# In a state-space scan, the carried part of a chunk is turned by two transposes ahead of its 64-column matmuls

## The chip, the cores and the metric

The kernel runs on one core of a Trainium2 chip. The core has engines that run side by side and meet only at semaphores: TensorE (PE in the profile, with PEld for its weight loads), VectorE (DVE), ScalarE (ACT), GpSimd (POOL) and SyncE (SP). The metric is the time of one execution on the device in microseconds (us); lower is better.

## The reference, cut to what matters

Two model blocks stand one behind the other: a two-layer block with differential attention, a linear recurrence and an MLP, then a block with a state-space scan over 768 tokens (256 of context, 512 latent) and an attention layer. The change is in the scan, which works in chunks of 128 tokens, in both directions of time:

```python
def ssd_scan(xs, dt, a, bm, cm, init_state, need_y=True):
    ...
    la_cum = jnp.cumsum(dtc * a, axis=2)
    to_end = jnp.exp(la_cum[:, :, -1:] - la_cum) * dtc
    states = jnp.einsum('bcsgn,bcsgr,bcsgrp->bcgrpn', bc, to_end, xc)
    chunk_decay = jnp.exp(la_cum[:, :, -1])

    def step(carry, inp):
        st, dec = inp
        return carry * dec[..., None, None] + st, carry

    final, prev = lax.scan(step, init_state.astype(F32), ...)
    ...
    cb = jnp.einsum('bclgn,bcsgn->bclsg', cc, bc)
    w = cb[..., None] * decay * dtc[:, :, None]
    y_diag = jnp.einsum('bclsgr,bcsgrp->bclgrp', w, xc)
    y_off = jnp.einsum('bclgn,bcgrpn,bclgr->bclgrp', cc, prev, jnp.exp(la_cum))
    return (y_diag + y_off).reshape(xs.shape), final
```

`y_off` is the carried part: what earlier chunks' states give to this chunk. `y_diag` is the part from within the chunk. There are 8 groups of 4 heads, each head 64 wide, and 6 chunks.

## The kernel before, in words

Every engine has its own program, in an order written out by hand. TensorE multiplies float32 data; the large products are made of float32r halves (`whi`, `wlo` and `inhi`, `inlo`), each product of them one pass, with three passes for one result. GpSimd splits each 1 MB weight tile into its halves (L337 and L341) as soon as TensorE is done with the tile that stood in that slot.

The scan runs over the 8 groups in `group(g, last)`: seven times in a hardware loop, and once more with `last` set. A group begins with a dense product for its gate (`zs`), then turns the convolved inputs of the 6 chunks (L692 to L694), makes the chunk states (L724), and goes through the 6 chunks. For each chunk c TensorE's order is: half a dense product for the next group (`next_half`, 24 matmuls of L628), the log decays of chunk c + 1 (L733, L735), `y_part(c)` (L757, L761), and the carried part of chunk c + 1 (`off_part`, L746). The last group has no next group, so its chunks have no dense product between them. Behind the chunks stand the output products of the group (`out_block`, again L628).

`y_part(c)` fills the 256 columns of one half of PSUM bank 7: two halves b of 128 columns, each 128 partitions high, where partitions 0 to 63 and 64 to 127 belong to two heads r. It waits for three semaphores: `offs_r` (the carried part of the chunk is in `offs`, laid out by token), `W_r` (the decay weights `wdec`) and `y_rd` (the bank's half was read). Then for each b it multiplies `offs` by the identity, a float32 product, which turns it from token rows to feature rows, and adds for each head r a product of 64 output partitions and 128 columns, `xcb` with `wdec`.

VectorE works in the order `gate_y(c - 1)` (L1926, reads bank 7), `offsets(c)` (L1917 to L1920, makes `offs`), `weights(c)` (L1903, L1907, makes `wdec`), with pieces of the next group's convolution (L1804, L1808), its activation (`silu`, L1822) and `skip` (L1899) placed among them. After chunk 5 it goes through `u_lo` (L1935), the remaining convolution, the eight additions to the output (`out_add`, L1997) and two sums of squares (L2002), and ends with `silu` of the last of four convolution blocks. TensorE may turn the next group's inputs (L692) only after that one.

Of the kernel before, what the change touches and what calls it, by code (L numbers as in the profile page):

```python
# [24 lines left out]
P = 128  # L25
# [69 lines left out]
def build(nc, io, stage=2):  # L95
# [258 lines left out]
    def _(pe):  # L354
# [74 lines left out]
        with pe.Fori(0, DEPTH) as l:  # L429
# [118 lines left out]
            b = 0  # L548
# [16 lines left out]
            for g in range(4):  # L565
                banks_wait(g % 2, ("pp_r", g + 1))
                for m in range(2):
                    n = 0
                    for kb in range(2):
                        c = kb * D + (2 * g + m) * P  # L570
                        for x, y in ((whi, phi), (wlo, phi), (whi, plo)):
                            mm = pe.matmul(ps[:, 2 * (g % 2) + m, :], x[:, T_PP % 2, c:c + P], y[:, kb, :],  # L572
                                           start=(n == 0), stop=(n == 5))
# [86 lines left out]
        for d, tri in enumerate((triF, triB)):  # L660
# [3 lines left out]
                  start=True, stop=True).then_inc(dt_p, 1)  # L664
        dense(T_BC0 % 2, lambda i: i * TM + P, P, IN, EIGHT, True, 0, lambda: pe.wait_ge(x_rd, 2))

        def group(g, last):
# [16 lines left out]
            for c in range(NC):  # L684
                q = 4 + c % 4
# [64 lines left out]
            def y_part(c):  # L750
                pe.wait_ge(offs_r, g * 6 + (c + 1))
                pe.wait_ge(W_r, g * 6 + (c + 1))
                pe.wait_ge(y_rd, g * 6 + (6 + c))
                base = (c % 2) * 256
                for b in range(2):
                    q = base + b * P
                    pe.matmul(ps[:, 7, q:q + P], offs[:, 0, 2 * b:2 * b + 2, :].rearrange("p r n -> p (r n)"), ident[:, :],  # L757
                              start=True, stop=False)
                    for r in range(2):
                        x0 = (2 * b + r) * HD  # L760
                        mm = pe.matmul(ps[64 * r:64 * r + 64, 7, q:q + P], xcb[:, c, x0:x0 + HD], wdec[:, 2 * b + r, :],  # L761
                                       start=False, stop=True)
                mm.then_inc(y_ps, 1)

            log_decay(0)
# [2 lines left out]
            for c, (name, part) in enumerate((("x0", 1), ("x1", 0), ("x1", 1), ("b", 0), ("b", 1), ("c", 0))):  # L768
                next_half(name, part)
                if c + 1 < NC:  # L770
                    log_decay(c + 1)
                y_part(c)
                if c + 1 < NC:
                    off_part(c + 1)
# [34 lines left out]
        for half in range(2):  # L809
            mm = pe.matmul(ps[:, 6 + half, 0:HALF], ones[:, :], acc[:, half * HALF:(half + 1) * HALF],  # L810
                           start=True, stop=True)
# [12 lines left out]
        for c in range(NC):  # L824
# [3 lines left out]
            for kb in EIGHT:  # L828
                for i, (a, w) in enumerate(((inhi, whi), (inhi, wlo), (inlo, whi))):
                    mm = pe.matmul(ps[:, 4 + c % 4, 0:TM], a[:, kb, cs], w[:, (T_ATT + 1) % 2, kb * TM:(kb + 1) * TM],  # L830
                                   start=(kb == 0 and i == 0), stop=(kb == KB - 1 and i == 2))
# [52 lines left out]
        for m in range(2):  # L884
            for half in range(2):
                mm = pe.matmul(ps[:, 4 + 2 * m + half, 0:HALF], bones[:, :], ksq[:, m, half * HALF:(half + 1) * HALF],
                               start=True, stop=True)
# [1533 lines left out]
```

## Time and profile before

| | |
|---|---|
| median of 3 runs | 2689.7 us (2688.63 to 2698.87) |
| the profiled execution | 2686.75 us |
| its span, first to last instruction | 2685.0 us |
| PE busy | 2454.4 us (91%) |
| DVE busy | 1433.8 us (53%) |
| POOL busy | 1308.4 us (49%) |
| ACT busy | 798.6 us (30%) |
| mean granted TensorE clock | 0.97 of full speed |

Times within the profile count from the start of the span. A float32 matmul that is a true product appears as two records, one for each pass; a float32 transpose appears as one. The duration of a record runs until its last result is out and overlaps with the records behind it, so what an instruction costs a stream of others is read from the distance between starts. In a row of the timeline, `x4` says that four neighbouring records of one kind are drawn together, and what stands in brackets is the engine's idle time ahead of it and what ended it.

### The profile page before, as it was taken

Reading aid. Unit: us, or ns where it says so; the run is one execution under the profiler, and the core shown is the slowest. Engines: PE = TensorE matmul, PEld = TensorE weight load, DVE = VectorE, ACT = ScalarE, POOL = GpSimd, SP = SyncE. Lnnn points to the kernel's source line nnn. Section 1 sums busy time; section 2 is a strip of 40 time slices with the busy share of each in tenths; the row PEclk is TensorE's granted clock in tenths of the full one; section 3 lists DMA queues with packets and bytes.
Section 4 is the critical chain, followed back from the end, with each engine's and each line's share of the span. In section 5 each row is a group of like instructions: output and inputs, shape, how many; then the busy total and the mean of one; then the engine's idle time right before and its main releaser. Section 6 shows DMA issues by size and latency. Waiting matters only on the chain.

```text
span 2685.0 us, 36345 instructions
## 1 busy us (share of the span) xinstructions
PE 2454.4 (91%) x13296; PEld 2033.1 (76%) x13296; DVE 1433.8 (53%) x1780; ACT 798.6 (30%) x1700; POOL 1308.4 (49%) x1220
## 2 busy tenths in 40 slices
PE   5989999999798899999977799999999997798997
PEld 4657888888665688888856698988898885676876
DVE  7574311114675541121356787778788786326762
ACT  2233110112222420011223333233333332325771
POOL 5734766667784276666762242443434341253003
PEclk9999999999899999999989899999999997999999
DMA  4211334432221034443231010110111112021001
GB/s 145 72 58 48 111 127 139 141 121 100 95 77 65 30 106 128 137 141 130 98 124 56 32 48 31 47 47 31 47 47 47 47 39 82 16 94 48 2 1 47
DMA packets 33839, 201.44 MB, mean 75 GB/s; under 512 B 4416, under 2 KB 6592, under 8 KB 13632
## 3 DMA queue, kind: packets, MB, share of 16 engines
q1 hardware_dynamic: 23328, 164.13, 17.5%
q10 hardware_dynamic: 10400, 35.73, 4.2%
q8 instruction: 82, 1.34, 0.2%
q14 instruction: 29, 0.24, 0.0%
HBM read 194.60 MB, written 5.24 MB: 74 GB/s over the span
## 4 chain that ended last, share of the span: by engine, by line
PE 82%; DVE 9%; ACT 4%; issue 3%; POOL 1%; DMA 0%; ACTq 0%; SPq 0%; DVEq 0%; POOLq 0%
PE ps L385 40%; PE ps L628 19%; PE ps L848 5%; PE ps L746 2%; PE ps L761 1%; PE ps L757 1%; PE ps L605 1%; PE ps L724 1%; PE ps L929 1%; PE ps L408 1%; PE ps L946 1%; PE ps L572 1%; PE ps L493 1%; ACT tin L1190 1%; PE ps L733 1%
## 5 line engine op out<-in xcount | busy, mean ns | idle before, releaser
L337 POOL TENSOR_SCALAR whi<-wraw 128x512 fp32r<-128x512 f32 x608 | 407.7, 698 | 1352.2 <-PE ps L628 628.2
L341 POOL TENSOR_TENSOR wlo<-wraw,whi 128x512 fp32r<-128x512 f32 x608 | 905.8, 1520 | 0.0
L385 PE MATMUL ps<-uhi,whi 128*128 128x512 f32 x960 | 383.9, 400 | 49.3 <-DVE ulo L1497 40.4
L385 PE MATMUL ps<-uhi,wlo 128*128 128x512 f32 x960 | 376.9, 393 | 0.0
L385 PE MATMUL ps<-ulo,whi 128*128 128x512 f32 x960 | 376.3, 392 | 0.0
L628 PE MATMUL ps<-inhi,whi 128*128 128x384 f32 (+1 forms) x816 | 258.2, 353 | 44.9 <-DVE inlo L1752 27.9
L385 PEld LDWEIGHTS ps<-uhi,whi 128*128 128x128 f32 x960 | 182.2, 190 | 94.8 <-issue 48.0
L628 PE MATMUL ps<-inhi,wlo 128*128 128x384 f32 (+1 forms) x816 | 246.1, 338 | 0.0
L628 PE MATMUL ps<-inlo,whi 128*128 128x384 f32 (+1 forms) x816 | 245.9, 338 | 0.0
L1670 DVE TENSOR_TENSOR h<-h,ps 128x1024 f32<-128x1024 f32 x40 | 48.9, 1221 | 306.4 <-PE ps L385 306.4
L385 PEld LDWEIGHTS ps<-uhi,wlo 128*128 128x128 f32 x960 | 182.3, 190 | 38.6 <-issue 1.9
L385 PEld LDWEIGHTS ps<-ulo,whi 128*128 128x128 f32 x960 | 182.0, 190 | 38.6
L385 PE MATMUL ps<-hidhi,whi 128*128 128x512 f32 x512 | 202.2, 395 | 0.0
L385 PE MATMUL ps<-hidhi,wlo 128*128 128x512 f32 x512 | 199.5, 390 | 0.0
L385 PE MATMUL ps<-hidlo,whi 128*128 128x512 f32 x512 | 199.3, 389 | 0.0
L628 PEld LDWEIGHTS ps<-inhi,whi 128*128 128x128 f32 (+1 forms) x816 | 150.8, 189 | 54.7 <-issue 40.4
L1282 ACT ACTIVATE ebuf<-ps,tabg 128x128 f32<-128x128 f32 x384 | 104.2, 383 | 170.7 <-PE ps L735 117.2
L628 PEld LDWEIGHTS ps<-inhi,wlo 128*128 128x128 f32 (+1 forms) x816 | 152.2, 190 | 2.1
L1687 DVE SCALAR_TENSOR_TENSOR hm<-ps,rstd 128x1024 f32<-128x1024 f32 x32 | 39.1, 1223 | 212.0 <-PE ps L385 212.0
L628 PEld LDWEIGHTS ps<-inlo,whi 128*128 128x128 f32 (+1 forms) x816 | 151.6, 189 | 0.9
L1808 DVE SCALAR_TENSOR_TENSOR convd<-raw,cpg,convd 128x770 f32<-128x770 f32 x128 | 146.3, 1143 | 2.3
L1131 ACT ACTIVATE hsq<-hm 128x1024 f32<-128x1024 f32 x32 | 34.0, 1061 | 296.5 <-DVE hm L1687 296.5
(369 smaller groups left out, 4519.0 us busy)
## 6 DMA issues: line engine op xcount, KB each, us to landing
wraw<-in_wstream SPq DMA_DIRECT2D x152, 1024.0 KB, 4.9
modraw<-in_modw ACTq DMA_DIRECT2D x48, 512.0 KB, 3.6
hspill<-hres ACTq DMA_DIRECT2D x1, 3072.0 KB, 9.4
hback<-hspill ACTq DMA_DIRECT2D x1, 3072.0 KB, 10.1
h<-in_x SPq DMA_DIRECT2D x1, 2048.0 KB, 7.4
out<-hfin SPq DMA_DIRECT2D x2, 1024.0 KB, 4.0
gw<-in_gates ACTq DMA_DIRECT2D x2, 512.0 KB, 5.3
pT<-in_pT ACTq DMA_DIRECT2D x2, 512.0 KB, 6.0
```

Of the source, the lines that this page charges most:

```text
L337: pool.tensor_scalar(whi[:, s, c], wraw[:, s, c], 1.0, 0.0, ALU.mult, ALU.add).then_inc(wraw_read, 1)
L341: ins = pool.tensor_tensor(wlo[:, s, c], wraw[:, s, c], whi[:, s, c].bitcast(F32), ALU.subtract)
L385: mm = pe.matmul(ps[:, 2 * bank + m, :], a[:, w, c:c + P], b[:, kb, :], start=(n == 0 and i == 0), stop=(n == KB - 1 and i == 2))
L408: mm = pe.matmul(ps[32 * j:32 * j + 2, 5, 0:P], cvec[:, kb, :], modraw[:, kb, :], start=(half == 0), stop=(half == 1))
L628: mm = pe.matmul(ps[0:width, q + half, 0:HALF], a[:, s, c:c + width], b[:, kb, half * HALF:(half + 1) * HALF], start=(n == 0), stop=(n == ...
L746: mm = pe.matmul(ps[:, 6, d * 256:(d + 1) * 256], ck[:, c * P:(c + 1) * P], ast[:, slot, :], start=True, stop=True)
L848: mm = pe.matmul(ps[:, q + m, :], a[:, k % 2, c:c + P], b[:, kb, t0:t0 + S], start=(kb == 0 and i == 0), stop=(kb == KB - 1 and i == 2))
L1131: A(hsq[n % 2][:, :, :], hm[n % 2][:, :, :], ACT.Square).then_inc(L["sqh_r"], 1)
L1282: ins = A(ebuf[:, d, r, :], ps[:, 4 + d, r * P:(r + 1) * P], ACT.Exp, bias=tabg[:, K_NB + 2 * c + d, r:r + 1])
L1670: V.tensor_tensor(h[:, 2 * j:2 * j + 2, :], h[:, 2 * j:2 * j + 2, :], TWO(bank), ALU.add).then_inc(L["h_r"], 1)
L1687: V.scalar_tensor_tensor(out=hm[n % 2][:, :, :], in0=TWO(n % 2), scalar=0.0, in1=rstd2, op0=ALU.max, op1=ALU.mult).then_inc(L["m_r"], 1)
L1808: ins = V.scalar_tensor_tensor(out=o, in0=r[:, n:n + CW], scalar=cpg[:, 6 * b + n:6 * b + n + 1], in1=o, op0=ALU.mult, op1=ALU.add)
```

## The change

Both halves of `offs` are turned first, one behind the other, with TensorE's transposing mode (`is_transpose=True`) in place of a product with the identity. Then come the four 64-column products that add to them. Only the first transposition clears the bank's accumulation state (`start=(b == 0)`), and the check on accumulation groups is told to leave the second half alone; neither of these two arguments adds an instruction.

```diff
                 for b in range(2):
                     q = base + b * P
                     pe.matmul(ps[:, 7, q:q + P], offs[:, 0, 2 * b:2 * b + 2, :].rearrange("p r n -> p (r n)"), ident[:, :],
-                              start=True, stop=False)
+                              start=(b == 0), stop=False, skip_group_check=(b == 1), is_transpose=True)
+                for b in range(2):
+                    q = base + b * P
                     for r in range(2):
                         x0 = (2 * b + r) * HD
                         mm = pe.matmul(ps[64 * r:64 * r + 64, 7, q:q + P], xcb[:, c, x0:x0 + HD], wdec[:, 2 * b + r, :],
-                                       start=False, stop=True)
+                                       start=False, stop=True, skip_group_check=(b == 1))
                 mm.then_inc(y_ps, 1)
```

In TensorE's order, chunk 0 of a group of the loop reads like this before (a line may stand for several instructions, xN; `mask_143` is the causal mask and `ident` the identity):

```order
L735 MATMUL ps<-lablk,lapick 128x512
L757 MATMUL ps<-ident,offs 128x128
L761 MATMUL ps<-wdec,xcb 64x128 x2
L757 MATMUL ps<-ident,offs 128x128
L761 MATMUL ps<-wdec,xcb 64x128 x2
L746 MATMUL ps<-ast,ck 128x256
```

and like this now, where L763 is the L761 of before:

```order
L735 MATMUL ps<-lablk,lapick 128x512
L757 MATMUL ps<-ident,offs 128x128 x2
L763 MATMUL ps<-wdec,xcb 64x128 x4
L746 MATMUL ps<-ast,ck 128x256
```

The number of instructions is the same, six; full-width and 64-column ones alternate no more. The other five chunks change alike, in the loop and in the last group. At chunk 5 the difference, the new text with + and the old with -, is

```order
 L753 REGISTER_ALU
-L757 MATMUL ps<-ident,offs 128x128
-L761 MATMUL ps<-wdec,xcb 64x128 x2
-L757 MATMUL ps<-ident,offs 128x128
-L761 MATMUL ps<-wdec,xcb 64x128 x2
+L757 MATMUL ps<-ident,offs 128x128 x2
+L763 MATMUL ps<-wdec,xcb 64x128 x4
 L628 MATMUL ps<-inhi,whi 128x384
```

where a dense product stands directly behind. No instruction of another engine moves, and no wait is added or taken away.

## Rows read from the trace of the kernel before

**Rows 1.** Chain that ended last, 1500 to 2250 us, shares by line

```profile
by line: PE ps L628 62.0%; PE ps L746 5.9%; PE ps L761 4.9%; PE ps L757 4.7%; PE ps L724 3.6%; issue 3.1%; PE ps L733 2.6%; PE ps L735 2.4%; DVE ebuf L1903 1.7%; DVE wdec L1907 1.5%; PE ps L692 1.3%; ACT ast L1273 1.3%; PE ps L693 1.1%; DVE
```

**Rows 2.** Lines L757, L761, L692: records, their duration in ns (min/median/max), first and last

```profile
L757 PE MATMUL ps<-ident,offs x192: 271/275/583, 1534.8 to 2241.9; 128*128 128x128 f32 x192
...
L761 PE MATMUL ps<-wdec,xcb x384: 272/323/477, 1535.1 to 2242.6; 128*64 128x128 f32 x192
...
L692 PE MATMUL ps<-ident,convd x96: 270/273/330, 1507.1 to 2188.8; 128*128 128x128 f32 x96
```

**Rows 3.** Timeline of PE, first chunk: start us, duration us, instruction, records

```profile
1534.79 0.38 PE L757 MATMUL ps<-ident,offs 128*128 128x128 f32 x2
1535.11 0.44 PE L761 MATMUL ps<-wdec,xcb 128*64 128x128 f32 x4
1535.48 0.49 PE L757 MATMUL ps<-ident,offs 128*128 128x128 f32 x2
1535.89 0.44 PE L761 MATMUL ps<-wdec,xcb 128*64 128x128 f32 x4
1536.26 0.70 PE L746 MATMUL ps<-ast,ck 128*128 128x256 f32 x2
```

**Rows 4.** Timeline of PE, transposes at a group's start

```profile
1507.06 0.38 PE L692 MATMUL ps<-ident,convd 128*128 128x128 f32 x2
1507.28 0.39 PE L693 MATMUL ps<-convd 128*128 128x128 f32 x2
```

**Rows 5.** Timeline of PE, sixteen 64-column passes in the attention stage

```profile
2522.82 1.09 PE L958 MATMUL ps<-ident,rrec 128*64 128x128 f32 x16
2523.84 0.44 PE L929 MATMUL ps<-ident,pexp 128*128 128x128 f32 x2
```

**Rows 6.** Waits of PE, 1500 to 2250 us: us in total, times, longest

```profile
PE ps L757 <- DVE wdec L1907: 9.0, 7, 1.3
```

**Rows 7.** Timeline of DVE, POOL and PE, chunks 1 to 3 of the first group

```profile
1543.55 0.42 DVE L1926 SCALAR_TENSOR_TENSOR zs<-ps,zs 128x256 f32<-128x256 f32 x1 [0.79 <-PE ps L761]
...
1546.77 0.69 DVE L1907 TENSOR_TENSOR wdec<-ebuf,xcb 128x512 f32<-128x512 f32 x1
...
1556.56 1.65 DVE L1907 TENSOR_TENSOR wdec<-ebuf,xcb 128x512 f32<-128x512 f32 x1
...
1551.82 5.84 POOL L341 TENSOR_TENSOR wlo<-wraw,whi 128x512 fp32r<-128x512 f32 x4
...
1558.45 0.48 PE L757 MATMUL ps<-ident,offs 128*128 128x128 f32 x2 [1.30 <-DVE wdec L1907]
```

**Rows 8.** Timeline of DVE and PE, from chunk 5 to the next group

```profile
1574.62 0.42 DVE L1926 SCALAR_TENSOR_TENSOR zs<-ps,zs 128x256 f32<-128x256 f32 x1
...
1581.82 0.95 DVE L1997 TENSOR_TENSOR oacc<-oacc,ps 128x768 f32<-128x768 f32 x1 [0.30 <-PE ps L628]
...
1601.64 2.04 DVE L1822 SCALAR_TENSOR_TENSOR convd<-raw,convd 128x770 f32<-128x770 f32 x1
...
1604.04 0.41 PE L692 MATMUL ps<-ident,convd 128*128 128x128 f32 x2 [0.21 <-issue]
```

**Rows 9.** Timeline of PE, last group: chunk 1 whole, chunk 3 its beginning

```profile
2213.53 0.73 PE L757 MATMUL ps<-ident,offs 128*128 128x128 f32 x2 [3.31 <-issue]
...
2216.18 0.80 PE L746 MATMUL ps<-ast,ck 128*128 128x256 f32 x1
...
2227.09 0.64 PE L757 MATMUL ps<-ident,offs 128*128 128x128 f32 x2 [2.16 <-issue]
```

**Rows 10.** Windows of PE: length us, busy us (records), granted clock, DMA share, GB/s

```profile
1657.00:1661.00 4.00, 4.00 (x14) 0.57 0.41 174
...
2452.00:2612.00 160.00, 145.01 (x1436) 0.98 0.03 8
```

**Rows 11.** Chain that ended last, behind chunk 3: first group, then second

```profile
1560.09 1.06 PE ps L746 x4
1561.15 4.16 PE ps L628 x24
...
1656.80 1.58 PE ps L746 x4
1658.39 5.25 PE ps L628 x24
```

## The prediction

> **What bounds the kernel now.** I read the chain that ended last first, over the stretch in which the scan runs. The reader sees that it is nearly all TensorE: 62.0% is dense products, and the two lines of `y_part` hold 4.7% and 4.9% [rows 1]. So the changed instructions lie on the path. The rows of the lines themselves say what they are: 192 records for L757, which are 8 groups x 6 chunks x 2 halves = 96 products of two passes each; 384 for L761 (192 products); and 96 for L692, which also does 8 x 6 x 2 = 96 turns, but in the transposing mode and with one pass each [rows 2]. Then I read the timeline for distances between starts, since durations of 0.27 us overlap. Last come the waits: in the scan `y_part` is late for VectorE once in a group, 1.3 us in chunk 3 (9.0 us in seven waits) [rows 6], because `wdec` takes 1.65 us instead of 0.69 while GpSimd subtracts [rows 7].
>
> **One y_part, step by step.** Before: it starts at 1534.79 and the next instruction at 1536.26, so 1.47 us [rows 3]. Its four pieces are 0.32 (two passes of the identity product and the step to 64 columns), 0.37 (four 64-column passes and the step back), 0.41 (the same as the first, but with its first weight load uncovered behind the step) and 0.37.
>
> After, the first piece is two transposes, one pass each. Two transposes cost 0.22 up to a full-width successor [rows 4], where no step to 64 columns follows; two full-width passes with the step cost 0.32 [rows 3]. As a transpose pass and a product pass have the same pitch of 0.11, I take 0.32. The second piece is eight 64-column passes. Sixteen of them with the step back take 2523.84 - 2522.82 = 1.02 us [rows 5], four take 0.37, so four more cost (1.02 - 0.37) / 3 = 0.22, and eight take 0.59. The sum is 0.91, and 1.47 - 0.91 = 0.56 us is saved per chunk. Of this 0.22 is two passes fewer for the transposes (two halves, one pass less each), and the rest, 0.34, comes from the order: one pair of steps between the widths instead of two.
>
> The ends for the one thing not shown, a transpose with a 64-column product behind it that adds to its columns: at the low end it is as cheap as two transposes with a full-width successor, 0.22, and 0.66 would be saved; at the high end each transpose costs what a record lasts, 2 x 0.27 = 0.54 in place of 0.32 [rows 2], and 0.34 is saved. I take 0.56, since the distances in rows 4 show that transposes overlap with their neighbours.
>
> The Trainium skill (TensorE: Matmul & The Clock Gate, Part 4: PE-mode transpose) gives about 275 ns for a transpose in a kernel's context. The duration of L692, 273 ns, agrees [rows 2], but the distance between starts does not bear out that this is its price in a stream; by the page's figure as a price the sum would be that of the high end.
>
> **What of it reaches the end.** The seven groups of the loop:
> - Chunks 0, 1, 2 and 4: TensorE does not wait ahead of `y_part`. What VectorE must deliver for the next chunk starts from the bank reads that TensorE releases, and moves with it. VectorE's own slack ahead of `gate_y` was 0.79 us in chunk 1 [rows 7], more than 0.56, so it does not become the bound there. 4 x 0.56 = 2.24.
> - Chunk 3: its start hangs on `wdec`, whose chain starts at the end of chunk 2's `y_part` and `off_part`, so it moves forward by 0.56; but GpSimd's 5.84 us of subtractions start at a time given by a dense product ahead of that `y_part`, and do not move against it. More of VectorE's work falls into them. VectorE runs there at 0.69 / 1.65 = 0.4 of its speed [rows 7], so up to 0.6 x 0.56 = 0.34 may be lost again; I take 0.2. The `y_part` of chunk 3 itself saves 0.56. Net 0.36 for this chunk.
> - Chunk 5: here VectorE is behind. It starts `gate_y(5)` at 1574.62 without having waited, and from there to the activation that ends at 1601.64 + 2.04 = 1603.68 it waits for TensorE once, for 0.30 us; TensorE then starts the next group's turns at 1604.04 after a wait [rows 8]. A faster `y_part(5)` can shorten that chain by 0.30 at most, and GpSimd, which TensorE releases earlier, eats some of it. I take 0.15, and expect TensorE's wait ahead of L692 to grow by about 0.4.
>
> That is 2.24 + 0.36 + 0.15 = 2.75 us for a group and 7 x 2.75 = 19.3 for the loop.
>
> The last group has no dense products between its chunks, and each `y_part` waits for work that the previous one released, so all of it is on the path. Chunks 1, 3 and part of 5 ran at the half clock: 2216.18 - 2213.53 = 2.65 us [rows 9] instead of 1.47. At that clock the new form is 0.32, 0.59 doubled, less what was already uncovered, some 1.7, and saves 0.95. So the six save 3 x 0.56 + 3 x 0.9 = 4.4, less 0.2 for chunk 1 behind GpSimd: 4.2.
>
> Sum: 19.3 + 4.2 = 23.5 us. The profiled execution of 2686.75 becomes 2663.3. The median of the runs shown is 3 us above that execution, 2689.7, and I predict against it: **2666 us**. Weight loads, other engines' instructions and all transfers are as before; the code's six instructions remain six, so issue costs nothing new. The second half's `start=False` changes a flag only.
>
> **The rivals.**
> 1. *VectorE takes over in the chunk loop.* For it: VectorE's slack of 0.79 shrinks to about 0.2, and chunk 3 is its already. Against it: chunks 1, 2 and 4 show an idle VectorE ahead of `gate_y`. If only three chunks of a group pay, it is 7 x 3 x 0.56 + 4.2 = 16 us, 2674.
> 2. *The clock falls, the rival on the slower side.* In the second group the granted clock is 0.57 between 1657 and 1661 us, right behind the wait of chunk 3 [rows 10], and the work there takes 1.58 and 5.25 us instead of 1.06 and 4.16 [rows 11]: one such stretch costs 1.6 us. If transposes in place of products weaken TensorE's activity so much that each of the loop's 42 `y_part`s is followed by one, that is 42 x 1.6 = 67 us against 23.5 saved: 2733. From 15 stretches on nothing is gained, from 23 on it is slower by over 0.5%. Against it: in the attention stage, with six transposes for each tile of scores, the clock is 0.98 [rows 10], and six of the seven waits of chunk 3 passed without a fall. The skill's same section says that transposing does not count as busy for the clock; by that rule this rival is live, and the attention row speaks against it. A milder form, seven stretches more, is 7 x 1.6 = 11 us, 2677.
> 3. *The change does not do all it says*: the transposes keep two passes, or cost their full duration. Two passes leave 0.34 per chunk, that is about 0.34 / 0.56 x 23.5 = 14 us, 2676; the high end of a transpose's cost gives the same. Against the first stand the 96 records of L692.
> 4. *All of it surfaces*, chunk 5 included: 48 x 0.56 + 1 = 28 us, 2662.
>
> **How the numbers follow.** The forecast has 0.66, its own range 2662 to 2671. Rival 1 has 0.12, rival 2 in its full form 0.03 and in its mild one 0.04, rival 3 has 0.08, rival 4 has 0.07. The range for 8 in 10 is 2658 to 2677: its low end is rival 4 with the cheapest transposes, its high end holds rivals 1 and 3. A measurement of this kernel tells 0.5%, 13 us, from no change; the border is 2676. Faster: 0.66 + 0.07 + 0.10 of rival 1 + 0.04 of rival 3 = 0.87. Same: 0.02 + 0.04 + 0.04 = 0.10. Slower: 0.03.
>
> **What would show it.** In the profile after: L757 with 96 records; distance from the first L757 to the next L746 or L628 of 0.91 us at full clock; the wait ahead of chunk 3's `y_part` still there, 1.3 to 1.6 us; the idle time ahead of the turns L692 up from 0.21 to about 0.6; the period of a group, from one L692 to the next, shorter by 2.75 us. The prediction is wrong if L757 keeps 192 records, if the distance is above 1.1 us, if VectorE appears as releaser of `y_part` in chunks 1, 2 or 4, or if there is more than one stretch of half clock in the loop's seven groups.

## The result and the profile after

The changed kernel takes 2677.3 us in the median of 6 runs (2674.9 to 2680.2), the one before 2696.8 in the median of its 6 (2688.6 to 2698.9). The ratio is 0.994, 95% interval 0.9925 to 0.9955: it is faster by some 16 us (12 to 20). The forecast was 2666, some 23.5 below the median of before that was known then (2689.7, three runs), with a range up to 2677; the time lies 0.3 us above that range. With three more runs the median of before is 7.1 us higher: its six runs lie at 2688.6 to 2689.7 (two) and at 2696.1 to 2698.9 (four).

The two profiled executions, 2686.75 and 2680.21 us, differ by less, and for a reason outside the change. The first chunk of the scan begins at 1534.79 before [rows 3] and at 1542.76 after, though up to there both programs have the same instructions. So the two traces are compared from that chunk on. Why that stretch took longer is read in the last section.

The lines themselves, with their records and durations in ns as in [rows 2]:

```profile
L757 PE MATMUL ps<-ident,offs x96: 270/271/466, 1542.8 to 2237.2; 128*128 128x128 f32 x96
...
L763 PE MATMUL ps<-wdec,xcb x384: 272/273/476, 1543.1 to 2238.2; 128*64 128x128 f32 x192
```

96 records for the transposes instead of 192. The timeline of TensorE (start and duration in us), at the first chunk of the first group and of the eighth:

```profile
1542.76 0.38 PE L757 MATMUL ps<-ident,offs 128*128 128x128 f32 x2
1543.07 0.66 PE L763 MATMUL ps<-wdec,xcb 128*64 128x128 f32 x8
...
2204.92 0.44 PE L757 MATMUL ps<-ident,offs 128*128 128x128 f32 x2 [1.55 <-DVE offs L1922]
2205.28 0.66 PE L763 MATMUL ps<-wdec,xcb 128*64 128x128 f32 x8
```

The turns take 0.31 up to the step to 64 columns, as worked out (0.32), and the whole `y_part` is 0.90 us in the trace (0.897 from its first start to the next instruction's), against 0.91 predicted. The seven groups of the loop take 2204.92 - 1542.76 = 662.2 us. Before, the same stretch ran from 1534.79 to 2207.04, 672.25 us. 10.1 us were saved where 19.3 were forecast. The last group, from its first chunk to the end of its last `y_part`, went from 35.9 to 33.7: 2.2 us instead of 4.2.

What holds TensorE up in the scan, first as waits in total (us, times, longest) and then the two places in the timeline that answer to [rows 7] and [rows 8]:

```profile
PE ps L757 <- DVE wdec L1909: 13.3, 7, 1.9
...
PE ps L692 <- DVE convd L1824: 3.2, 6, 0.6
```

```profile
1558.66 5.82 POOL L341 TENSOR_TENSOR wlo<-wraw,whi 128x512 fp32r<-128x512 f32 x4
...
1559.05 1.18 DVE L1921 TENSOR_TENSOR offs<-offs 128x256 f32<-128x256 f32 x1
...
1563.40 1.63 DVE L1909 TENSOR_TENSOR wdec<-ebuf,xcb 128x512 f32<-128x512 f32 x1
...
1565.27 0.43 PE L757 MATMUL ps<-ident,offs 128*128 128x128 f32 x2 [1.90 <-DVE wdec L1909]
...
1610.98 0.41 PE L692 MATMUL ps<-ident,convd 128*128 128x128 f32 x2 [0.52 <-DVE convd L1824]
```

Chunk 3 waits 1.90 us, not 1.30, and not the 1.3 to 1.6 of the forecast. It starts 1565.27 - (1558.66 + 5.82) = 0.79 us behind the end of GpSimd's subtractions; before it was 1558.45 - (1551.82 + 5.84) = 0.79 too [rows 7]. Where the time went is seen in the second row above, VectorE's first piece on `offs` within the subtractions. This is the row of before that answers to it:

```profile
1552.80 0.59 DVE L1919 TENSOR_TENSOR offs<-offs 128x256 f32<-128x256 f32 x1
```

It started 0.98 us behind the start of GpSimd's subtractions; now it starts 0.39 behind it, takes 1.18 us instead of 0.59, and ends 1.57 behind it as before. The three pieces behind it take 1.40, 1.77 and 1.63 us, against 1.40, 1.77 and 1.65 before. So what VectorE starts earlier, it loses beside GpSimd.

And the granted clock falls behind that wait in six of the seven groups, where it did in one before [rows 11]. The windows of TensorE (length, busy us and records, granted clock, DMA share, GB/s), one behind each chunk 3 (1.00 is full clock; 0.66 is a part of the window at half clock and the rest at full):

```profile
1565.00:1570.00 5.00, 4.73 (x21) 0.66 0.65 213
1661.00:1666.00 5.00, 5.00 (x23) 0.66 0.61 210
1756.00:1761.00 5.00, 4.29 (x19) 0.66 0.61 210
1852.00:1857.00 5.00, 4.49 (x20) 0.66 0.61 210
1947.00:1952.00 5.00, 3.75 (x16) 0.66 0.60 210
2043.00:2048.00 5.00, 4.03 (x18) 0.66 0.61 210
2139.00:2144.00 5.00, 4.27 (x28) 1.00 0.59 210
```

A group with a fall takes 95.7 to 95.8 us from chunk 0 to chunk 0, and from chunk 3 to chunk 4 it needs 8.61; the seventh group, without one, needs 7.03. One fall costs 1.6 us.

### The profile page after: what moved, and what is told of

It reads as the page before. It is cut to its first block, busy times and chain, and to the rows that moved or that the text cites. A ratio compares the mean times of both kernels' runs of the same rounds, so it can differ in the third digit from the quotient of the medians.

```text
span 2678.3 us, 36153 instructions
## 1 busy us (share of the span) xinstructions
PE 2442.2 (91%) x13200; PEld 2025.8 (76%) x13200; DVE 1444.3 (54%) x1780; ACT 798.8 (30%) x1700; POOL 1314.4 (49%) x1220
## 3 DMA queue, kind: packets, MB, share of 16 engines
q1 hardware_dynamic: 23328, 164.13, 17.6%
## 4 chain that ended last, share of the span: by engine, by line
PE 74%; DVE 15%; issue 5%; ACT 4%; POOL 1%; DMA 0%; ACTq 0%; DVEq 0%; SPq 0%; POOLq 0%
PE ps L385 40%; PE ps L628 11%; PE ps L850 5%; DVE convd L1810 3%; PE ps L746 2%; PE ps L605 1%; PE ps L724 1%; PE ps L763 1%; PE ps L493 1%; PE ps L408 1%; PE ps L931 1%; PE ps L948 1%; DVE convd L1824 1%; PE ps L572 1%; ACT tin L1192 1%
```

## The experiments

Ten experiments were run; e7 is the changed kernel once more. The scan's loop, from chunk 0 of the first group to chunk 0 of the eighth, is read in each trace from the starts of those two `y_part`s; it excludes what comes ahead, which varies by itself (last section). Falls are those of the granted clock within these seven groups. Each ratio is to runs of before made beside that kernel, whose median was 2696.8, 2690.7 (e1 to e4), 2694.0 (e5 to e8) and 2694.9 us (e9, e10); so medians of different rows are compared by their ratios. The waits and falls come from one trace for each kernel.

| kernel | loop us | y_part us | wait ahead of chunk 3 | falls | median of all runs, ratio to before |
|---|---|---|---|---|---|
| before | 672.25 | 1.47 | 1.30 | 1 | 2696.8, 1 |
| changed | 662.2 | 0.90 | 1.90 | 6 | 2677.3, 0.994 |
| e1 transposes, old order | 662.0 | 1.20 | 1.61 | 0 | 2684.2, 0.9975 |
| e2 products, new order | 661.8 | 1.12 | 1.64 | 1 | 2681.7, 0.9967 |
| e3 wait filled, products | 652.5 | 0.90 | 0.2 | 0 | 2675.2, 0.9939 |
| e4 wait filled, transposes | 652.5 | 0.90 | 0.2 | 0 | 2666.9, 0.991 |
| e5 GpSimd released later | 648.8 | 0.90 | none (1.0 to 1.15 at chunk 4) | 0 | 2665.6, 0.9897 |
| e6 dense half split | 642.7 | 0.90 | none | 0 | 2656.4, 0.986 |
| e7 changed, again | 662.15 | 0.90 | 1.90 | 6 | 2678.1, 0.9947 |
| e8 only chunk 2 changed | 677.0 | 1.47 | 1.9 | 4 | 2691.1, one run |
| e9 split, old y_part | 663.1 | 1.47 | none | 0 | 2680.4, 0.9959 |
| e10 chunk 5 as before | 663.8 | 0.90 | 1.90 | 6 | 2676.5, one run |

**e1, the transposes alone.**

```diff
-                              start=True, stop=False)
+                              start=(b == 0), stop=False, skip_group_check=True, is_transpose=True)
                     for r in range(2):
...
```

> The transposes alone, in the order of before (each half turned, then its two products). Pass theory: a y_part loses two passes and keeps all four steps between widths, 1.47 - 0.22 = 1.25 us. The wait ahead of chunk 3 grows from 1.30 to 1.52. Theory L (the clock falls because TensorE waits 1.9 us for VectorE in chunk 3, not because of what the transposes are): fewer falls in the loop's seven groups than the six of the changed kernel, 1 to 3. Theory T (transposes do not count as work for the clock): six or seven falls, as in the changed kernel, since the transposes are the same. Time: some 9 us below before with few falls, about 0 to 2 us below it with seven.

**e2, the order alone.** The changed kernel without `is_transpose=True`.

> The order alone: both products with the identity first, then the four 64-column products. y_part 1.47 - 0.36 = 1.11 us, so the order carries 0.36 of the 0.57 saved. The wait ahead of chunk 3 grows from 1.30 to about 1.66. Theory T: no more falls of the clock in the loop than before (0 to 2), and some 14 us below before. Theory L: falls come back with the wait, 2 to 6, and the gain is 14 us less 1.6 for each.

The timelines of TensorE, e1 first:

```profile
1548.37 0.27 PE L757 MATMUL ps<-ident,offs 128*128 128x128 f32 x1
1548.57 0.44 PE L761 MATMUL ps<-wdec,xcb 128*64 128x128 f32 x4
1548.94 0.33 PE L757 MATMUL ps<-ident,offs 128*128 128x128 f32 x1
1549.19 0.44 PE L761 MATMUL ps<-wdec,xcb 128*64 128x128 f32 x4
1549.56 0.48 PE L746 MATMUL ps<-ast,ck 128*128 128x256 f32 x1
```

```profile
1540.42 0.61 PE L757 MATMUL ps<-ident,offs 128*128 128x128 f32 x4
1540.96 0.66 PE L763 MATMUL ps<-wdec,xcb 128*64 128x128 f32 x8
```

e1 takes 1549.56 - 1548.37 = 1.19 us for a `y_part` (1.20 in the table, from unrounded starts) and saves 0.27, where 0.22 was expected; e2 takes 1.12 and saves 0.35. Together in one kernel they save 0.57, a little less than the sum of the two. So both parts work, the order somewhat more. Both loops are as short as the changed one, because they have no or one fall. e1 is against theory T: it has the changed kernel's transposes and no fall. But e2 is no help to theory L, which expected 2 to 6 falls from its wait of 1.64 us: it has one, within the 0 to 2 of theory T. And e1's groups of 95.5 us follow each other almost as the falls of the changed kernel do (95.6 us apart), so that its seven waits stand at nearly the same place against the clock's changes. The two runs together do not decide between the theories; e3 and e4 do.

**e3 and e4, the wait filled.** Extra work ahead of chunk 3's `y_part`, its results unused, goes into PSUM bank 3, which is free there:

```diff
+                if c == 3 and not last:
+                    for n in range(10):
+                        pe.matmul(ps[:, 3, 0:HALF], whi[:, SB, 0:P], inhi[:, 0, 0:HALF], start=True, stop=True)
                 y_part(c)
```

and in e4 instead

```diff
+                if c == 3 and not last:
+                    for n in range(4):
+                        for i in range(4):
+                            pe.transpose(ps[:, 3, i * P:(i + 1) * P], ident[:, :], ident[:, :])
                 y_part(c)
```

> The changed kernel, with ten extra float32r passes of 384 columns (10 x 0.17 = 1.7 us) into a free bank ahead of chunk 3's y_part, in the time in which TensorE waits. Their results are not used. If the wait is what lets the clock fall (theory L): no falls in the loop, 6 x 1.6 = 9 us below the changed kernel. If it is the transposes (theory T): falls stay, time as the changed kernel.

> The same place filled with 16 transposes of the identity (16 x 0.11 = 1.76 us), results unused. If transposes count as TensorE's activity, it behaves as the kernel filled with products: no falls, 9 us below the changed kernel. If they do not count (theory T, the rule on the transposing mode), the six falls stay and the time is the changed kernel's.

e4's timeline of TensorE at chunk 3, and the window of its loop behind that of the changed kernel:

```profile
1555.79 1.91 PE L777 MATMUL ps<-ident 128*128 128x128 f32 x16
1557.90 0.43 PE L757 MATMUL ps<-ident,offs 128*128 128x128 f32 x2 [0.20 <-DVE wdec L1913]
```

```profile
1542.80:2204.90 662.10, 639.40 (x3726) 0.98 0.13 44
```

```profile
1535.30:2187.90 652.60, 642.03 (x3839) 1.00 0.13 45
```

Chunk 3 starts no earlier (22.51 us behind chunk 0 in the changed kernel, 22.5 to 22.6 in both of these), TensorE does more, and the loop is 9.6 us shorter: six falls at 1.6. Alignment doesn't explain it: groups of 94.1 to 94.2 us against 95.6 put the seven chunks 3 of each trace at seven different places, and none is followed by a fall. The falls come with the idle wait, and sixteen transposes in a row, 1.9 us of them, keep the clock up as well as ten products do. Theory T is refuted.

In whole runs e4 shows the gain (ratio 0.991) and e3 does not: its 0.9939 is the changed kernel's 0.994, where 9 us less were expected. In its profile the stretch ahead of the scan ended 4.0 us later than in that of the changed kernel (1546.78 against 1542.76), which hides a part; where the rest is, no run shows.

**e5, GpSimd released later.** The tile that TensorE finishes ahead of chunk 2's `y_part` ("x1") is given back behind that `y_part`:

```diff
-            if 1 in parts:
+            if 1 in parts and last is not None:
...
-                "x1": (SX, P, True, 0, lambda: pe.wait_ge(x_rd, g * 4 + 5)),
+                "x1": (SX, P, None, 0, lambda: pe.wait_ge(x_rd, g * 4 + 5)),
...
                         mm = pe.matmul(ps[:, 6, d * 256:(d + 1) * 256], ck[:, c * P:(c + 1) * P], ast[:, slot, :],
                                        start=True, stop=True)
+                        if c == 3 and d == 0 and not last:
+                            mm.then_inc(tile_done, 1)
```

> The changed kernel, but the weight tile that TensorE finishes ahead of chunk 2's y_part is handed back to GpSimd only at the first product of chunk 3's carried part, some 1.2 us later. Theory G (chunk 3's start is set by the end of GpSimd's subtractions, so chunk 2's y_part saves nothing and the wait grew from 1.30 to 1.90): VectorE makes offs and wdec of chunk 3 ahead of the subtractions, wdec takes about 0.7 us instead of 1.63, the wait of 1.90 us goes, and with it the falls of the clock; the loop from first to eighth group, 662.2 us in the changed kernel, becomes 662.2 - 7 x 1.9 - 6 x 1.6 = 639 us, and the kernel some 22 us faster than the changed one. Rival V (VectorE's own chain sets chunk 3's start, GpSimd only goes on beside it): the wait stays near 1.9 us and the loop at 662 us.

The timelines of VectorE, GpSimd and TensorE there:

```profile
1552.83 1.09 DVE L1907 TENSOR_TENSOR ebuf<-ebuf 128x512 f32<-128x512 f32 x1
1553.95 1.66 DVE L1911 TENSOR_TENSOR wdec<-ebuf,xcb 128x512 f32<-128x512 f32 x1
...
1553.35 6.92 POOL L341 TENSOR_TENSOR wlo<-wraw,whi 128x512 fp32r<-128x512 f32 x4
...
1555.86 0.44 PE L759 MATMUL ps<-ident,offs 128*128 128x128 f32 x2
...
1564.18 0.43 PE L759 MATMUL ps<-ident,offs 128*128 128x128 f32 x2 [1.15 <-DVE wdec L1911]
```

The wait of 1.90 is gone, chunk 3 starts 20.55 us behind chunk 0 instead of 22.51, and no clock falls. `wdec` still takes 1.66 us, where 0.7 was expected, but it now ends 1560.27 - 1555.61 = 4.66 us ahead of the end of GpSimd's subtractions; in the changed kernel it ended 0.55 behind it. Now the same subtractions lie on VectorE's next pieces, and a wait of 1.15 us comes back ahead of chunk 4. So chunk 3's wait does hang on when GpSimd subtracts, as theory G says, but the gain in the loop is 13.4 us, not the 23 expected (639 us): contention that was moved, not removed.

**e6, the dense half split.** Of the half ahead of chunk 4 ("b", part 1), the first 12 matmuls go ahead of chunk 3's `y_part`; `dense` got an argument for a range of its k blocks.

```diff
-                next_half(name, part)
+                next_half(name, part, (4, KB) if c == 4 else None)
                 if c + 1 < NC:
                     log_decay(c + 1)
+                if c == 3:
+                    next_half("b", 1, (0, 4))
                 y_part(c)
...
```

> The changed kernel, with the first 12 of the 24 dense matmuls of the half that stands ahead of chunk 4 moved ahead of chunk 3's y_part: real work in the wait, 12 x 0.17 = 2.1 us. If the wait only lets the clock fall and TensorE's work is the bound, TensorE is free earlier in chunk 4 and the group gains up to 1.9 us, plus no falls: loop 662 - 13 - 9 = 640 us. If VectorE sets the pace from chunk 3 on (its work for chunk 4 starts only behind chunk 3's y_part), a wait comes back ahead of chunk 4's y_part, and the group gains 0.5 to 1.3 us besides the falls: loop 644 to 649 us.

```profile
1571.26 0.43 PE L760 MATMUL ps<-ident,offs 128*128 128x128 f32 x2
...
1576.67 0.43 PE L760 MATMUL ps<-ident,offs 128*128 128x128 f32 x2 [0.32 <-DVE wdec L1914]
```

Chunk 3 starts where it did, 22.51 behind chunk 0, without a wait; chunk 4 follows 5.4 us later instead of 7.03, with a wait of 0.32 only. The loop is 642.7, better than the 644 expected for the slower case. At 2656.4 us in the median of four runs (ratio 0.986, interval 0.9842 to 0.9879) this version beats both kernels; the changed kernel, run beside it as e7, took 2678.1 (0.9947).

**e7, the changed kernel again.**

> The changed kernel once more, on this chip. If six falls of the clock in the loop's seven groups belong to the kernel (wait of 1.9 us ahead of chunk 3), this profile shows five to seven again and a loop of about 662 us. If they were the chance of one execution, it shows 0 to 3 and a loop of 653 to 657 us, as in the profile with the filled wait.

Six falls and a loop of 662.15 us: they belong to the kernel.

**e8, only chunk 2 changed.** The other five `y_part`s in the form of before.

> Only chunk 2's y_part in the new form, the other five as before. Theory G: chunk 3 still starts where GpSimd's subtractions end, so the start of chunk 3 relative to chunk 0 stays at 23.66 us, the wait grows from 1.30 to about 1.87, and a group's period stays at 96.7 us (no fall counted). Rival V: chunk 3 starts 0.57 us earlier, at 23.09, and the period is 96.2.

```profile
1552.51 5.82 POOL L341 TENSOR_TENSOR wlo<-wraw,whi 128x512 fp32r<-128x512 f32 x4
...
1559.12 0.48 PE L762 MATMUL ps<-ident,offs 128*128 128x128 f32 x2 [1.86 <-DVE wdec L1913]
```

Chunk 3 starts 23.62 us behind chunk 0 (23.66 before), again 1559.12 - 1558.33 = 0.79 behind GpSimd's end. The groups without a fall take 96.71 to 96.75, as before. What chunk 2 saves is lost whole. And with the longer wait (1.86 to 1.91 us) there are four falls instead of one, so this kernel is slower in the loop by 4.8 us than the one before.

**e9, the split without the change.** e6 with the old `y_part`.

> The kernel before (old y_part) with the dense half ahead of chunk 4 split, 12 matmuls ahead of chunk 3's y_part, as in e6. If VectorE and GpSimd set the pace of chunks 3 and 4, the wait of 1.3 us is filled with 2.1 us of work, so TensorE arrives 0.8 us late at chunk 3, and the group gains about 1 us (period 95.7 instead of 96.7, no falls) : the loop about 665 us against 642.7 with both changes. Then the change of y_part is worth about 22 us in the loop once the wait is filled, more than the 17.6 (672.2 - 1.6 to 662.2 - 9.6 us) that it was worth by itself without the falls. If split and change simply add, the loop is 642.7 + 17.6 = 660 us.

663.1 us against e6's 642.7: behind a filled wait the change is worth 20.4 us in the loop, twice the 10.1 that it brought alone. That lies between the two cases expected, 17.6 if split and change only add and 22 if VectorE and GpSimd set the pace. The split alone is worth 9.1 us in the loop, nearly as much as the change alone.

**e10, chunk 5 as before.**

```diff
+                new = c != 5
```

> The changed kernel, with chunk 5's y_part in the old form (0.57 us longer). If VectorE's chain from chunk 5 to the next group's turns is the bound there, as the prediction had it, the stretch from chunk 5 to the next group's chunk 0 (58.55 us in the changed kernel) grows by 0.15 to 0.3 us only, and the wait ahead of the turns L692 shrinks from 0.52 to about 0.2. If TensorE is the bound, it grows by 0.57.

```profile
1606.45 0.41 PE L692 MATMUL ps<-ident,convd 128*128 128x128 f32 x2 [0.21 <-issue]
```

From chunk 5's start to the turns L692 it takes 31.33 us, 31.07 in the changed kernel and 31.33 before. The `y_part` is 0.57 longer, the stretch 0.26, and the wait ahead of L692 is 0.21 again: both as expected if VectorE's chain is the bound there. Less than half of a longer `y_part` reaches the next group.

## Why the prediction came out as it did

The direction was right, and so were the mechanism and the price of a `y_part`; the sum was not, mainly because of the clock.

The time missed its range for two reasons. The first is in the traces: the scan gained 12.3 us where 23.5 were forecast, and 8 of the missing 11.2 are falls of the clock. The second is the starting point: 23.5 was taken from a median of three runs, 2689.7, and six runs have 2696.8. Without the first the time would be some 2669, and the ratio of 0.994 on 2689.7 gives 2674, so with either one right it would have come inside the range. That the miss is just 0.3 us is chance. The medians also show a larger gain (16 by the ratio) than the scan in the two traces. In this pair 2.3 us more lie behind the scan, from the end of the last `y_part` to the end of the span (442.1 before, 439.8 after); that stretch has the same instructions and takes 439.1 to 442.2 us over all twelve traces, so this is not credited to the change.

- *One y_part*: 0.56 saved in the forecast, 0.573 measured, with both parts shown (e1, e2). The high bound, a transpose at the duration of its record, 0.27, is refuted: e1's turn costs 0.20 with the step to 64 columns.
- *Chunks 0, 1 and 4*: between the chunks' starts 0.54 (0 to 1), 0.60 (1 to 2) and 0.60 (4 to 5) were saved, and no wait for VectorE came ahead of these `y_part`s. Right; rival 1 did not take over.
- *Chunks 2 and 3*: the term was 0.56 for chunk 2, less 0.2 for GpSimd. Measured is nothing for chunk 2: chunk 3 starts 9.01 us behind it before and after (e8 shows the same alone). My bound of 0.34 came from a speed ratio, 0.69 / 1.65. In fact VectorE's pieces ended at the same times against GpSimd's subtractions although they could start earlier (the row of 0.59 us that became 1.18), and chunk 3 starts 0.79 us behind the end of these in all three traces. So the wait grew by the whole 0.6 us, to 1.90, past the 1.3 to 1.6 named ahead. Chunk 3's own `y_part` saved 0.59.
- *Chunk 5*: 0.15 forecast, 0.25 measured; the wait ahead of L692 grew to 0.52, not the 0.6 forecast. Right in kind (e10).
- These make 2.58 us for a group without falls instead of 2.75, and 18.1 for the loop instead of 19.3.
- *The clock*: this is the step that failed. The forecast carried over the one fall of before. It had named the mechanism and its price, 1.6 us (1.6 measured), but gave seven more of them a chance of 0.04 and nothing in the sum, with the argument that six of seven waits had passed without. That was an argument from a wait of 1.30 us, applied to one that the change would make longer. One of the forecast's own signs of being wrong, more than one stretch of half clock in the loop, came true. Five more falls cost 8 us: 18.1 - 8 = 10.1, the measured gain of the loop.
- *The last group*: 2.2 instead of 4.2. TensorE stands idle ahead of each of its chunks, and its clock goes up and down in both traces, at other chunks in each; two chunk spacings grew (5.76 to 6.58, 5.75 to 6.07). This was not tried apart.

The sum is 23.5 - 8 - 1.2 - 2.0 = 12.3 us, which is what the traces show from the first chunk to the end of the scan. The rule of the Trainium skill (TensorE: Matmul & The Clock Gate, Part 4: PE-mode transpose) that transposing does not count as busy for the clock named the risk, but not its cause: by it e4 should have kept its six falls, and it had none.

What stays open is which of these waits lets the clock fall. Their length seems to count: before and e8 differ in chunk 2's `y_part` alone, 1.3 against 1.9 us of wait, and have one and four falls, in one trace each. But length isn't all. The seven waits of the changed kernel are all 1.90 or 1.91 us, and one has no fall. Its first and its sixth fall (windows as above), which begin 0.83 us behind chunk 3's start at 1565.27 and 0.03 behind that at 2043.97:

```profile
1566.10:1569.50 3.40, 3.40 (x13) 0.51 0.67 275
...
2044.00:2047.40 3.40, 3.40 (x15) 0.50 0.87 296
```

The falls are 95.6 us apart and the groups 95.7, so the chunks move by 0.1 to 0.2 us a group against the falls, and in the seventh, where a fall at that step would begin at 2139.6, ahead of chunk 3's start at 2139.73, it is missing. e7 repeats this, and in e10, whose groups are 96.0 us, it is the fourth group that has none. So the place of a wait against the clock's changes counts beside its length. Which place and which length it takes no experiment varied apart, and the few falls of e1 and e2 (waits of 1.61 and 1.64 us) may come from either.

## What to carry to other kernels

Where full-width and 64-column matmuls alternate, the steps between them cost time: here one pair of steps fewer saved 0.35 of 1.47 us (e2). So group by width, and turn with the transposing mode, which saved 0.27 (e1). Before counting a shorter piece as time saved, look behind it for a wait that another engine sets, here GpSimd's subtractions beside VectorE: the gain ahead of it is lost. And when a wait grows, price the clock that may fall behind it; filling the wait with work that is due anyway (e6) paid both back.

## What the runs showed of the hardware

The stretch ahead of the scan, the same instructions in every kernel, ended between 1534.8 and 1548.8 us in the profiles. The granted clock over it differs. The windows from 0 to 1480 us of before, of the changed kernel and of e6, whose first chunks began at 1534.79, 1542.76 and 1548.75:

```profile
0.00:1480.00 1480.00, 1354.72 (x6632) 0.98 0.30 102
```

```profile
0.00:1480.00 1480.00, 1356.27 (x6586) 0.97 0.30 102
```

```profile
0.00:1480.00 1480.00, 1358.76 (x6576) 0.96 0.30 101
```

That is 14 us of spread between executions, more than the change brought. The lower the granted clock over this stretch, the later the scan began, in all twelve traces. e3 and e4 have the same loop to 0.1 us, and medians that differ by 8. A stretch of the trace that holds the change told in one profile what some ten runs of the whole did not.
